# Context copy ahead of the next head's exponential on ScalarE, and output stores issued by SyncE

## The chip, the cores and the metric

The program runs on one core of a Trainium2 chip. The time is device microseconds (us) of one execution. Three timed executions of the kernel before gave 4782.5 us as their median (4778.81 to 4790.28). In the profile the engines are PE (TensorE matmuls), PEld (TensorE weight loads), DVE (VectorE), ACT (ScalarE), POOL (GpSimd) and SP (SyncE, which here only issues DMAs).

## The reference, cut to what matters

The program computes one layer: projections, two kinds of attention (a sliding-window one, "window", and one over at most 256 selected keys, "latent"), a gated mix, and a SwiGLU block. The change lies in the attention. Cut down, the latent branch is:

```python
rel   = relu(einsum('bqhd,bsd->bqhs', q_idx, k_idx))       # index scores, 8 heads
score = einsum('bqh,bqhs->bqs', w_idx, rel)                # masked by chunk, then top_k(score, 256)
q_lat = einsum('bqhd,hrd->bqhr', q, w_uk)                  # "absorbed" query
logits = einsum('bqhr,bqkr->bhqk', q_lat, c_sel) * scale - slope * dist
p   = softmax(logits)                                      # over the selected keys
ctx = einsum('bhqk,bqkr->bqhr', p, c_sel)                  # "context"
o   = einsum('bqhr,hrd->bqhd', ctx, w_uv)
```

The window branch computes a softmax over 16 + 128 keys with a sink, and its product with V. Both outputs go to a DRAM tensor, `attn`, which the last stage reads.

## The kernel before

Four stages follow each other, with a barrier between them: projection, key preparation, `attention` (busy from about 1138 to 2755 us of the profiled execution) and `mix_and_ffn`. Only `attention` is changed.

`attention` works through 16 tiles of 128 queries, and in each tile through 8 heads: 128 steps, n = 8 t + h. A tile t has 16 + 128 (t+1) visible keys, so the steps grow. There is no scheduler: each engine has its own program, written by hand as one loop over n, and the engines meet through semaphores. An engine executes its instructions in order, so whatever waits holds up everything behind it on that engine.

In step n the engines do this:

- **PE**: transposes the first two items of step n (an item is a window piece, in heads 3 to 6, or a group of four key blocks of the latent probabilities), with up to two buffers `turn` in PSUM; then index scores for 32 steps ahead (`index`, tiles up to 11 only); then the first block of logits for step n+2 (`logits`, matmuls at L94 to L96); then `weigh` of item 0, which multiplies the copied transposes with the values (L926 for a window item, L931 for a latent one). It goes on with the transpose of item 2, `weigh` of item 1, the further blocks of logits, and the remaining items. The first latent `weigh` of a step waits for `ctx_free` (the context of step n-1 has been copied out of its only PSUM buffer) and every `weigh` waits for `turn_free` (ACT has copied this item's transposes into `p_t`). In head 0 the step ends with the transpose of the finished window output (L942) and `expand` (L949: context times w_uv for the previous tile); in head 2 with the transpose of the latent output.
- **ACT**: `latent_exp(n+1)` (L1049, waits for DVE's `u_ready`; PE needs it only for the transposes of step n+1); in head 1 `evacuate_product(1, t-1)` (L1079, waits for `expand`); `evacuate_context(n-1)` (L1075, waits until the last `weigh` of step n-1 has ended); in heads 2 to 5 `window_exp` (L1055, L1057); then the first count of the search for the k-th score (`tally`, L1043, which waits for POOL); then `evacuate` of items 0 and 1 (L1069, copies transposes to `p_t`), `rectify` (L1021), the second count, the other items, and the third count. At the end of heads 0 and 2 it runs `store`: a copy of the transposed output into `o_t` (L1088), a drain, and the DMA to `attn` (L1090), issued by ACT itself.
- **DVE** adds distances to logits (L1268), sums index scores, and counts for the search in the even tile of a pair. **POOL** judges each count (L777) and gives the next candidate. The counts run in even tiles (2, 4, ..., heads 1 to 7) and in the first three heads of odd ones, and in tile 0, but not in tiles 14 and 15.
- **SP** loads each tile's inputs: `load_qb`, `load_qi`, `load_window` and `load_values`.

Of the kernel before, what the change touches and what calls it, by code (L numbers as in the profile page):

```python
# [25 lines left out]
P = 128  # L26
# [18 lines left out]
START = 1  # L45
# [11 lines left out]
TILES = SEQ // P  # L57
# [440 lines left out]
def attention(nc, proj, v_nat, w_uk, w_uv, sinks, attn, keys):  # L498
# [4 lines left out]
    with Scope(nc, "at") as s:  # L503
# [59 lines left out]
        sink_used = s.sem("sink_used")  # L563
        stats_a, exp_a, raw_ready, o_ready, attn_stored = s.sem("stats_a"), s.sem("exp_a"), s.sem("raw_ready"), s.sem("o_ready"), s.sem("attn_stored")
        count_ready, sign_ready, cand_ready, kth_ready = s.sems("count_ready"), s.sems("sign_ready"), s.sems("cand_ready"), s.sems("kth_ready")
# [70 lines left out]
        with nc.Block() as block:  # L636
            @block.sync
            def _(sp):
# [31 lines left out]
                def load_values(t):  # L670
# [4 lines left out]
                    sp.dma_start(v_win[:, 1, :], v_nat[w0 + WH - META:w0 + WH - META + WH, :]).then_inc(v_loaded, 16)  # L675

                load_qi(0)
                load_qb(0)
# [4 lines left out]
                for t in range(TILES - 1):  # L683
                    load_qb(t + 1)
                    if t + 5 < TILES:
                        load_qi(t + 5)
                    load_window(t + 1)
                    load_values(t + 1)

            @block.gpsimd  # L690
# [308 lines left out]
            def _(act):  # L999
# [84 lines left out]
                def store(branch, t):  # L1084
                    u, k = turn_at["out", t, branch]
                    act.wait_ge(turn_ready[u], k + 1 + START)
                    act.wait_ge(attn_stored, 32 * t + START)
                    act.activation(o_t[branch][:, :, :], turn[u][:, :].rearrange("p (j q) -> p j q", j=4), ACT.Copy).then_inc(turn_free[u], 1)  # L1088
                    act.drain()
                    act.dma_start(attn[branch * 512:branch * 512 + 512, t * P:t * P + P].rearrange("(j p) c -> p j c", p=P),  # L1090
                                  o_t[branch][:, :, :]).then_inc(attn_stored, 16)

# [7 lines left out]
                for n in range(STEPS):  # L1100
# [5 lines left out]
                    if searches(n, 0):  # L1106
                        orient(q)
                    if n + 1 < STEPS:
                        latent_exp(n + 1)
                    if h == 1 and t:  # L1110
                        evacuate_product(1, t - 1)
                    if n:
                        evacuate_context(n - 1)
                    if searches(n, 0):
                        flip(q)
# [31 lines left out]
                store(1, TILES - 1)  # L1147
                act.wait_ge(attn_stored, 32 * TILES + START)

# [641 lines left out]
```

## Time and profile before

| | |
|---|---|
| Median of three timed executions | 4782.5 us |
| The profiled execution's own time | 4787.24 us |
| Its span in the profile | 4785.4 us |
| PE busy | 3987.3 us (83%) |
| PEld busy | 3309.6 us (69%) |
| ACT busy | 1707.0 us (36%) |
| DVE busy | 1524.6 us (32%) |
| POOL busy | 1534.7 us (32%) |
| Mean granted clock of TensorE | 0.893 of full speed |

An engine's busy time is the union of its instructions' times. In a row of the timeline the first number is the start, the second the duration, both in microseconds; brackets give the engine's idle time just before and what released it. A row with x8 merges eight instructions. Two neighbouring instructions of ACT overlap by about 0.1 us in these rows, so what one occupies of the engine is the distance from its start to the start of the next.

### The profile page before, as it was taken

The page shows a single profiled execution, that of the slowest core. Times are in us where ns is not written, and L with a number is a line of the kernel's source. Part 1 is how long each engine was busy: PE and PEld are TensorE (multiplying, and loading weights), DVE is VectorE, ACT ScalarE, POOL GpSimd, SP SyncE. Part 2 cuts the span into 40 slices and gives each one's busy share as a digit, 9 for nine tenths or more (in the row PEclk, how much of TensorE's full clock was granted, in tenths as well). Part 3 has the DMA queues.
Part 4 walks back from the last instruction along what each step waited for, and adds up shares of the span by engine and source line. Part 5 has one row for each costly group of instructions (what it writes and reads, how often), then busy time and mean ns, then how long its engine had stood idle before and what let it go on. Part 6 is the DMA issues. An engine that isn't in the chain of part 4 may idle for free. (4 is left out here: it accounts for less than half of the span.)

```text
span 4785.4 us, 56614 instructions
## 1 busy us (share of the span) xinstructions
PE 3987.3 (83%) x19153; PEld 3309.6 (69%) x19153; DVE 1524.6 (32%) x2432; ACT 1707.0 (36%) x2775; POOL 1534.7 (32%) x1991
## 2 busy tenths in 40 slices
PE   2999999935677777777778868998899889988998
PEld 2888888714565666666667756886688768876886
DVE  7000000034455666666664213103210331023111
ACT  1000121114556666666664423422242224322221
POOL 2101011023444342323230033444444434453443
PEclk9999999955667888888889988999899989998999
DMA  4111212121100000000000042334233423333332
GB/s 159 53 57 62 66 53 66 57 53 24 31 18 24 25 16 17 17 16 12 12 12 13 7 160 75 96 114 150 70 96 114 132 92 96 115 107 117 96 94 87
DMA packets 368443, 321.21 MB, mean 67 GB/s; under 512 B 18120, under 2 KB 327528, under 8 KB 364168
## 3 DMA queue, kind: packets, MB, share of 16 engines
q1 hardware_dynamic: 344400, 292.72, 20.3%
q10 hardware_dynamic: 23872, 26.29, 1.6%
q8 instruction: 97, 1.59, 0.1%
q14 instruction: 74, 0.61, 0.0%
HBM read 258.79 MB, written 60.17 MB: 67 GB/s over the span
## 5 line engine op out<-in xcount | busy, mean ns | idle before, releaser
L1468 POOL TENSOR_TENSOR ff_w_lo<-ff_raw,ff_w_hi 128x1024 fp32r<-128x1024 f32 x328 | 794.8, 2424 | 1015.3 <-ACT ff_w_hi L1515 1015.3
L94 PE MATMUL ff_bank<-ff_h_hi,ff_w_lo 128*128 128x512 f32 x1664 | 660.4, 397 | 97.1 <-POOL ff_w_lo L1468 81.4
L95 PE MATMUL ff_bank<-ff_h_hi,ff_w_hi 128*128 128x512 f32 x1664 | 656.6, 395 | 0.0
L96 PE MATMUL ff_bank<-ff_h_lo,ff_w_hi 128*128 128x512 f32 x1664 | 655.6, 394 | 0.0
L1515 ACT ACTIVATE ff_w_hi<-ff_raw 128x1024 fp32r<-128x1024 f32 x328 | 345.9, 1055 | 762.2 <-PE ff_bank L96 750.5
L931 PE MATMUL at_ctx<-at_p_t,keys_c_nat 128*128 128x128 f32 (+1 forms) x2432 | 418.7, 321 | 153.2 <-ACT at_p_t L1069 152.2
L931 PEld LDWEIGHTS at_ctx<-at_p_t,keys_c_nat 128*128 128x128 f32 (+1 forms) x2432 | 368.8, 225 | 191.7 <-issue 159.4
L94 PEld LDWEIGHTS ff_bank<-ff_h_hi,ff_w_lo 128*128 128x128 f32 x1664 | 318.1, 191 | 174.7 <-issue 108.4
L94 PE MATMUL in_acc<-pj_h_hi,in_w_lo 128*128 128x512 f32 x1024 | 418.5, 409 | 11.9 <-POOL in_w_lo L300 11.9
L96 PE MATMUL in_acc<-pj_h_lo,in_w_hi 128*128 128x512 f32 x1024 | 416.8, 407 | 0.0
L95 PE MATMUL in_acc<-pj_h_hi,in_w_hi 128*128 128x512 f32 x1024 | 416.5, 407 | 0.0
L94 PE MATMUL ff_bank<-ff_w_hi,ff_f_lo 128*128 128x512 f32 x960 | 374.5, 390 | 7.7 <-POOL ff_w_lo L1468 4.1
L96 PE MATMUL ff_bank<-ff_w_lo,ff_f_hi 128*128 128x512 f32 x960 | 373.6, 389 | 0.0
L95 PE MATMUL ff_bank<-ff_w_hi,ff_f_hi 128*128 128x512 f32 x960 | 373.5, 389 | 0.0
L1043 ACT ACTIVATE at_equal<-at_score,at_cand 128x528 bf16<-128x528 f32 (+6 forms) x217 | 297.9, 1373 | 209.9 <-POOL at_cand L780 152.2
L96 PEld LDWEIGHTS ff_bank<-ff_h_lo,ff_w_hi 128*128 128x128 f32 x1664 | 317.9, 191 | 67.7
L95 PEld LDWEIGHTS ff_bank<-ff_h_hi,ff_w_hi 128*128 128x128 f32 x1664 | 318.2, 191 | 65.5
L1200 DVE TENSOR_SCALAR_CACHE_REDUCE at_greater<-at_score,at_cand 128x400 bf16<-128x400 f32 (+6 forms) x217 | 309.9, 1428 | 111.0 <-POOL at_cand L780 71.2
L300 POOL TENSOR_TENSOR in_w_lo<-in_raw,in_w_hi 128x1024 fp32r<-128x1024 f32 x32 | 76.7, 2399 | 729.6 <-ACT in_w_hi L307 729.6
L1069 ACT ACTIVATE at_p_t<-at_turn 128x512 f32<-128x512 f32 (+4 forms) x416 | 212.6, 539 | 198.1 <-PE at_turn L909 179.8
L858 PE MATMUL at_big_i<-keys_ki_hi,at_qi 128*128 128x512 f32 (+4 forms) x352 | 173.6, 493 | 90.4 <-POOL at_qi L716 73.6
L94 PEld LDWEIGHTS in_acc<-pj_h_hi,in_w_lo 128*128 128x128 f32 x1024 | 200.1, 195 | 59.5 <-issue 12.3
(233 smaller groups left out, 6217.0 us busy)
## 6 DMA issues: line engine op xcount, KB each, us to landing
ff_raw<-in_w_ff_gate SPq DMA_DIRECT2D x88, 512.0 KB, 3.8
ff_raw<-in_w_ff_up SPq DMA_DIRECT2D x88, 512.0 KB, 3.8
ff_raw<-in_w_ff_down SPq DMA_DIRECT2D x88, 512.0 KB, 3.6
proj<-in_row SPq DMA_DIRECT2D x32, 1032.0 KB, 4.7
in_raw<-in_w_in SPq DMA_DIRECT2D x32, 512.0 KB, 5.8
ff_gates<-proj SPq DMA_DIRECT2D x64, 256.0 KB, 2.8
ff_raw<-in_w_out SPq DMA_DIRECT2D x32, 512.0 KB, 3.7
ln_x<-in_x SPq DMA_DIRECT2D x16, 512.0 KB, 3.2
```

The source lines that it names most:

```text
L94: pe.matmul(out, lhs_lo, rhs_hi, start=start, stop=False)
L95: pe.matmul(out, lhs_hi, rhs_hi, start=False, stop=False)
L96: return pe.matmul(out, lhs_hi, rhs_lo, start=False, stop=stop)
L300: pool.tensor_tensor(w_lo[u][:, :, :], raw[u][:, :, :], f32(w_hi[u][:, :, :]), ALU.subtract).then_inc(lo_ready[u], 1)
L858: pe.matmul(big_i[:, a:a + n], qi_2[:, h, :], ki_hi[:, cols], start=True, stop=False)
L931: last = pe.matmul(ctx[:, 0, :], c_nat[0:rows, a:a + P], p_t[v][0:rows, m, :], start=(a == 0), stop=(a + rows == w))
L1043: act.activation(equal[:, 0:width(t)], score_of(t), ACT.Sign, bias=one(cand, 1), accum_out=one(count, 1)).then_inc(count_ready[1], 1)
L1069: act.activation(p_t[v][0:rows, 0:many, :], turn[u][0:rows, 0:many * P].rearrange("p (m q) -> p m q", m=many), ACT.Copy).then_inc(turn_fre ...
L1200: dve.tensor_scalar(greater[:, 0:width(t)], score_of(t), one(cand, 0), None, ALU.is_ge, ALU.add, accum_out=one(count, 0)).then_inc(count_r ...
L1468: pool.tensor_tensor(w_lo[u][:, :], raw[u][:, :], f32(w_hi[u][:, :]), ALU.subtract).then_inc(lo_ready[u], 1)
L1515: act.activation(w_hi[u][:, :], raw[u][:, :], ACT.Copy).then_inc(hi_ready[u], 1)
```

## The change

On ACT, `latent_exp(n + 1)` moves behind `evacuate_product(1, t - 1)` and `evacuate_context(n - 1)`. And the DMA of `store` moves to SP: ACT only counts up a new semaphore `out_ready` after the drain, and SP waits for it. SP's stores of tile t-1 stand between `load_window(t + 1)` and `load_values(t + 1)`, those of the last two tiles at the end, and so does the wait for their landing, which ACT had before.

```diff
+                def store(branch, t):
+                    sp.wait_ge(out_ready, 2 * t + branch + 1 + START)
+                    sp.dma_start(attn[branch * 512:branch * 512 + 512, t * P:t * P + P].rearrange("(j p) c -> p j c", p=P),
+                                 o_t[branch][:, :, :]).then_inc(attn_stored, 16)
...
                     load_window(t + 1)
+                    if t:
+                        store(0, t - 1)
+                        store(1, t - 1)
                     load_values(t + 1)
+                for t in (TILES - 2, TILES - 1):
+                    store(0, t)
+                    store(1, t)
+                sp.wait_ge(attn_stored, 32 * TILES + START)
...
                     act.drain()
-                    act.dma_start(attn[branch * 512:branch * 512 + 512, t * P:t * P + P].rearrange("(j p) c -> p j c", p=P),
-                                  o_t[branch][:, :, :]).then_inc(attn_stored, 16)
+                    act.sem_inc(out_ready, 1)
...
-                    if n + 1 < STEPS:
-                        latent_exp(n + 1)
                     if h == 1 and t:
                         evacuate_product(1, t - 1)
                     if n:
                         evacuate_context(n - 1)
+                    if n + 1 < STEPS:
+                        latent_exp(n + 1)
...
-                act.wait_ge(attn_stored, 32 * TILES + START)
```

ACT's instructions at the end of tile 15's head 0 and the start of its head 1, before (`at_o_t` is the output's copy, `at_u_b` the exponential, `at_o_nat` the product's copy, `at_ctx_t` the context's, `at_p_t` the copies that `weigh` reads):

```order
L1069 ACTIVATE at_p_t<-at_turn 16x128
L1088 ACTIVATE at_o_t<-at_turn 128x512
L1090 DMA attn<-at_o_t 128x4x128
L1049 ACTIVATE at_u_b,at_den_b<-at_u_b,at_min_b 128x2064
L1079 ACTIVATE at_o_nat<-at_misc 128x512
L1075 ACTIVATE at_ctx_t<-at_ctx 128x128
L1069 ACTIVATE at_p_t<-at_turn 128x512 x4
```

The same place on ACT in the changed kernel, where the lines have moved by 12:

```order
L1081 ACTIVATE at_p_t<-at_turn 16x128
L1100 ACTIVATE at_o_t<-at_turn 128x512
L1091 ACTIVATE at_o_nat<-at_misc 128x512
L1087 ACTIVATE at_ctx_t<-at_ctx 128x128
L1061 ACTIVATE at_u_b,at_den_b<-at_u_b,at_min_b 128x2064
L1081 ACTIVATE at_p_t<-at_turn 128x512 x4
```

The DMA is gone from ACT, and the exponential, which was first, is now behind the copy that waits for `expand` and the one that waits for the last `weigh`.

ACT at the start of tile 15's head 4, before:

```order
L1069 ACTIVATE at_p_t<-at_turn 16x128
L1049 ACTIVATE at_u_b,at_den_b<-at_u_b,at_min_b 128x2064
L1075 ACTIVATE at_ctx_t<-at_ctx 128x128
L1057 ACTIVATE at_u_a,at_den_a<-at_u_a,at_bias_a 128x208 x2
L1069 ACTIVATE at_p_t<-at_turn 104x512
```

And in the changed kernel:

```order
L1081 ACTIVATE at_p_t<-at_turn 16x128
L1087 ACTIVATE at_ctx_t<-at_ctx 128x128
L1061 ACTIVATE at_u_b,at_den_b<-at_u_b,at_min_b 128x2064
L1069 ACTIVATE at_u_a,at_den_a<-at_u_a,at_bias_a 128x208 x2
L1081 ACTIVATE at_p_t<-at_turn 104x512
```

The two have changed places; the first copy that `weigh` reads (104x512) stays behind both.

## Rows read from the trace of the kernel before

**Rows 1.** Three stretches: length, then busy time of each engine, PEclk, DMA share, GB/s.

```profile
1138.00:2300.00 1162.00, 846.69 (x4589) 720.95 (x4590) 718.98 (x1121) 710.56 (x1388) 433.56 (x1226) 0.79 0.07 19
2300.00:2549.00 249.00, 187.31 (x1141) 166.65 (x1140) 161.81 (x187) 153.53 (x239) 65.03 (x203) 0.85 0.05 13
2549.00:2765.00 216.00, 174.55 (x1249) 153.48 (x1247) 52.16 (x96) 93.59 (x182) 16.41 (x17) 0.96 0.06 21
```

**Rows 2.** Waits from 1138 to 2765 us: total us, times, longest.

```profile
POOL at_step L777 <- DVE at_greater L1200: 253.2, 98, 8.5
...
PE at_ctx L931 <- ACT at_p_t L1069: 152.2, 48, 9.3
```

**Rows 3.** Context copy: durations (ns); ACT's idle before it; who waited (us, times).

```profile
L1075 ACT ACTIVATE at_ctx_t<-at_ctx x128: 250/256/279, 1148.5 to 2746.4; 128x128 f32<-128x128 f32 x128
...
  PE at_ctx L931: 6.2, 7
...
  PEld at_ctx L931: 127.3, 27
```

**Rows 4.** Timeline of PE and ACT, tile 8, head 4 to 5: start, duration.

```profile
1900.09 1.74 PE L931 MATMUL at_ctx<-at_p_t,keys_c_nat 128*128 128x128 f32 x12
...
1903.82 1.26 ACT L1049 ACTIVATE at_u_b<-at_u_b,at_min_b 128x1168 f32<-128x1168 f32 x1
```

**Rows 5.** Timeline of PE and ACT, tile 15, head 3 to 4.

```profile
2704.85 1.47 PE L931 MATMUL at_ctx<-at_p_t,keys_c_nat 128*128 128x128 f32 x10
...
2705.22 2.00 ACT L1049 ACTIVATE at_u_b<-at_u_b,at_min_b 128x2064 f32<-128x2064 f32 x1
...
2707.22 0.25 ACT L1075 ACTIVATE at_ctx_t<-at_ctx 128x128 f32<-128x128 f32 x1
...
2708.28 1.05 ACT L1069 ACTIVATE at_p_t<-at_turn 104x512 f32<-104x512 f32 x2
...
2708.91 1.10 PE L926 MATMUL at_misc<-at_v_win,at_p_t 104*128 104x64 f32 x8 [0.18 <-ACT at_p_t L1069]
```

**Rows 6.** The same in tile 14, head 3 to 4.

```profile
2602.37 2.20 PE L931 MATMUL at_ctx<-at_p_t,keys_c_nat 128*128 128x128 f32 x16
...
2603.07 1.90 ACT L1049 ACTIVATE at_u_b<-at_u_b,at_min_b 128x1936 f32<-128x1936 f32 x1
...
2606.02 1.07 ACT L1069 ACTIVATE at_p_t<-at_turn 104x512 f32<-104x512 f32 x2
...
2606.82 1.00 PE L926 MATMUL at_misc<-at_v_win,at_p_t 104*128 104x64 f32 x8
```

**Rows 7.** Timeline of PE and ACT, tile 15, end of head 0 and head 1.

```profile
2665.98 1.90 PE L949 MATMUL at_misc<-at_wuv,at_ctx_t 128*128 128x64 f32 x16
...
2666.84 0.38 ACTq L1090 DMA_DIRECT2D attn<-at_o_t  x1
2667.27 2.02 ACT L1049 ACTIVATE at_u_b<-at_u_b,at_min_b 128x2064 f32<-128x2064 f32 x1 [0.49 <-issue]
...
2669.29 0.58 ACT L1079 ACTIVATE at_o_nat<-at_misc 128x512 f32<-128x512 f32 x1
...
2670.05 0.28 ACT L1075 ACTIVATE at_ctx_t<-at_ctx 128x128 f32<-128x128 f32 x1 [0.18 <-issue]
2670.22 1.08 ACT L1069 ACTIVATE at_p_t<-at_turn 128x512 f32<-128x512 f32 x2
...
2670.95 1.13 PE L931 MATMUL at_ctx<-at_p_t,keys_c_nat 128*128 128x128 f32 x8 [0.80 <-ACT at_p_t L1069]
```

**Rows 8.** Timeline of PE and ACT, tile 15, end of head 2 and head 3.

```profile
2692.64 2.02 ACT L1049 ACTIVATE at_u_b<-at_u_b,at_min_b 128x2064 f32<-128x2064 f32 x1 [0.50 <-issue]
...
2696.44 0.74 PE L926 MATMUL at_misc<-at_v_win,at_p_t 104*128 104x64 f32 x5 [2.13 <-ACT at_p_t L1069]
```

**Rows 9.** Timeline of PE and ACT, tile 9, head 7.

```profile
2048.90 1.49 ACT L1049 ACTIVATE at_u_b<-at_u_b,at_min_b 128x1424 f32<-128x1424 f32 x1 [2.89 <-DVEq L1271]
...
2051.28 0.91 PE L931 MATMUL at_ctx<-at_p_t,keys_c_nat 128*128 128x128 f32 x6 [0.51 <-ACT at_p_t L1069]
```

More of the change, by code:

```diff
@@ L563, in attention @@
         sink_used = s.sem("sink_used")
-        stats_a, exp_a, raw_ready, o_ready, attn_stored = s.sem("stats_a"), s.sem("exp_a"), s.sem("raw_ready"), s.sem("o_ready"), s.sem("attn_stored")
+        stats_a, exp_a, raw_ready, o_ready, out_ready, attn_stored = s.sem("stats_a"), s.sem("exp_a"), s.sem("raw_ready"), s.sem("o_ready"), s.sem("out_ready"), s.sem("attn_stored")
         count_ready, sign_ready, cand_ready, kth_ready = s.sems("count_ready"), s.sems("sign_ready"), s.sems("cand_ready"), s.sems("kth_ready")
```

## The prediction

> **What bounds the kernel now.** I read the busy time by stretch first, then the waits of the attention stage, then the timeline of ACT and PE side by side. The first view shows that in the attention no engine is full: from 1138 to 2300 us PE is busy 846.7 of 1162 us, and DVE and ACT about 710 each [rows 1]. So the time is a chain that goes from engine to engine. From 2549 us (tiles 14 and 15) PE is busy 174.6 of 216 us and ACT 93.6. The waits say where the chain changes engine: PE stood 152.2 us in 48 places before a latent `weigh` until ACT had made `p_t`, and POOL 253.2 us in 98 places for DVE's count [rows 2]. PE waits for `p_t`; what ACT does ahead of the first `p_t` copy of a step is therefore on the path, unless PE still has logits to do.
>
> **What the exchange does in one step.** Both copies and the exponential stand ahead of the first `p_t` copy in both orders, so no work leaves that piece; only where ACT waits can change. The exponential waits for DVE's `u_ready`, the context copy for PE's last `weigh` of the step before, and the head-1 product copy for `expand`. Three cases follow.
>
> (1) Both inputs are long there when ACT arrives. Tile 8's head 4 is typical: the last `weigh` ended at 1900.09 + 1.74 = 1901.83, the exponential began at 1903.82 [rows 4]. The exchange costs nothing. I compared the 128 steps one by one; in some 80, nearly all steps with a search, it is so.
>
> (2) ACT arrives before PE has finished. Before, the exponential covered that wait: ACT idled only 6.2 us in 7 of 128 steps ahead of the context copy [rows 3]. Now ACT waits first and then does the exponential. Tile 15, head 4: the exponential began at 2705.22, while the last `weigh` ended at 2704.85 + 1.47 = 2706.32. The new exponential begins at 2706.32 + 0.03 (semaphore) + 0.16 (what the copy occupies), and the copy's 0.16 behind it is saved, so everything behind both is late by 2706.35 - 2705.22 = 1.13 us. PE's L926 already waited (0.18) for the `p_t` copy [rows 5], so PE loses the whole 1.13. In tile 14 the same reckoning gives 2602.37 + 2.20 + 0.03 - 2603.07 = 1.53; PE had 2606.82 - 2606.55 - 0.1 = 0.17 us of cover there (first copy's end 2606.55 from two copies in 1.07 us at 2606.02, 0.1 the usual hop), which leaves 1.36 [rows 6].
>
> The steps where PE is then late, each reckoned like this: tile 15, heads 2, 4, 5, 6: 4 x 1.13 = 4.5. Tile 14, heads 4 and 5: 2 x 1.37; head 2: 0.7; heads 6 and 7, where PE's logits cover about 1.0 of 1.53: 2 x 0.55; 4.5 together. Tile 13, heads 2, 5, 6: 0.3 + 1.3 + 0.45 = 2.1. Five small ones in tiles 1, 5, 6 and 10: 1.0. In tiles 3, 5, 11 and the rest of 1, ACT is late by 0.2 to 0.7 too, but PE's index scores and logits cover it (0.5 to 4 us), so nothing. Sum: +12.1 us.
>
> Head 1 is its own place. The product copy now comes before the exponential and needs `expand`, which in tile 15 ends at 2665.98 + 1.90 = 2667.88. Then 0.03 + 0.76 (product copy with its drain, 2670.05 - 2669.29) + 0.17 (context, 2670.22 - 2670.05) + 2.02 (exponential with its read, 2669.29 - 2667.27) give 2670.86 for the first `p_t` copy, against 2670.22 before: +0.64, and PE waited 0.80 for it [rows 7]. Tiles 4 to 12 (even), 14 and 15 read alike at 0.62 to 0.69, tile 2 with 0.3 left after its cover: 7 x 0.65 + 0.3 = +4.9 us. In odd tiles to 13 `expand` ends 2 to 5 us before ACT gets there: nothing.
>
> (3) DVE is late: ACT waits for `u_ready` and the context is ready. Then the context copy slips into the wait and its 0.16 goes off the path. Tile 9's head 7 is such a step: 2.89 us of wait for DVE, and PE waited 0.51 for `p_t` [rows 9]. There are nine with PE waiting (tiles 7, 9, 11, 13): 9 x -0.16 = -1.4 us.
>
> **The stores.** ACT's gap between the output copy and the next instruction is 0.49 to 0.50 us, of which the DMA issue takes 0.38 [rows 7, 8]. With drain and semaphores alone the gap is 0.18 (behind the product copy, the row of L1075 in rows 7). So 0.32 us can go per store. It does go where nothing else is late: after head 2 in tiles 3 to 15, 13 times; in head 3 of tile 15 PE waited 2.13 us for ACT [rows 8]. After head 0 it goes nowhere: in even tiles and 15 the product copy now waits for `expand`, in odd ones the count waited 0.8 to 4 us for POOL anyway. The last two stores change only who issues. 13 x -0.32 = -4.2 us; the bounds are 0 and 32 x -0.38 = -12.2. On SP the stores hold up `load_values(t+1)`, which waits for head 6 anyway, later than the store's head 2, and the next tile's loads stand behind that: no cost. The transfers are the same, so no bandwidth changes (the DMA share is 0.05 to 0.07 [rows 1]). [...]
>
> **Sum.** 12.1 + 4.9 - 1.4 - 4.2 = +11.4 us. The profiled execution took 4787.24 and would become 4798.6; it lay 4.7 above the median of the three timed ones, so I put the change on the median: 4782.5 + 11.4 = 4794.
>
> **The rivals.**
> - *Absorbed.* The delays of ACT are real, but the chain through DVE and POOL gives most of them back: in the search steps POOL waits for DVE's count (253.2 us [rows 2]), not for ACT's. Against it: tiles 14 and 15 have no search, and there PE waits for ACT directly [rows 5]. If a third of the 17.0 us comes through: 5.7 - 1.4 - 4.2 = about 0: 4783. At zero it is 4777.
> - *Context gate, the faster side.* PEld waited 127.3 us in 27 places for the context copy [rows 3]. If that single PSUM buffer is what holds PE, the copy comes earlier by one exponential, 1.26 to 2.0 us [rows 4, 5], say 1.3 x 27 = 35 us, and with the stores the time is 4782.5 - 35 - 4.2 = 4743. It decides only if the context copy is the last thing PE needs. Against it: it is only the weight load that waits there; the matmul needs `p_t`, which ACT makes after the context copy in both orders, and all rows of PE's matmuls name `p_t` as the releaser [rows 5, 7, 9].
> - *The clock falls.* [...] If the new waits bring the last stretch to 0.85, its 174.6 us of PE become 174.6 x 0.96/0.85 = 197, +22 if all of it is on the path, about half of that by the share of steps bound by ACT: 11.4 + 12 = 4806. Against it: PE's 2.13 us wait in tile 15 [rows 8] is longer than the new ones of about 1.3. [...]
>
> That SP does not issue the stores in time is no case of its own: a tile passes before `o_t` is reused.
>
> **Chances.** Forecast 0.53 (own range 4788 to 4800), absorbed 0.27, clock 0.14, context gate 0.06. The range 4779 to 4808 takes in the forecast, nearly all of absorbed and the clock's middle. A measurement of this kernel tells from no change what is over about 0.2%, 9.6 us; the forecast's 11.4 is just beyond it, and two thirds of its cases are. Slower: 0.53 x 0.63 + 0.14 = 0.48 with rounding. Same: 0.53 x 0.37 + 0.27 less a little = 0.45. Faster: 0.07.
>
> **What would show it.** In the changed profile ACT's idle before the context copy should grow from 6.2 us in 7 steps to some 40 to 60 us in about 40, most in tiles 13 to 15; the idle of PE before L926 and L931 in tile 15's heads 4 and 5 from 0.2 to about 1.3, and each of those steps 1.1 us longer; the gap behind the output copy from 0.49 to about 0.18. The step in head 1 of the even tiles should be 0.6 longer. If tiles 14 and 15 together are not 9 to 11 us longer, the reckoning of case (2) is wrong; if tiles 2 to 12 move by more than some 5 us either way, it is the clock or the search chain, which I did not resolve; if the context copies come earlier and PE's matmuls with them, the gate was real.

## The result and the profile after

| | Kernel before | Changed kernel |
|---|---|---|
| Median | 4784.66 us (8 runs, 4778.81 to 4790.28) | 4805.4 us (8 runs, 4795.36 to 4808.05) |
| Span of the profiled execution | 4785.4 us | 4803.6 us |
| Mean granted clock of TensorE | 0.893 | 0.892 |
| ACT busy | 1707.0 us | 1707.9 us |

The changed kernel takes 1.0040 times as long (95% interval 1.0029 to 1.0051): +20.7 us. It was timed again in a later series and gave 4803.65 against 4787.69, 1.0031 (1.0019 to 1.0043): +16.0 us. The forecast was +11.4. No engine has more work (PE x19153, DVE x2432, ACT x2775 and POOL x1991 instructions in both traces; PE busy 3987.3 us before and 3991.2 us after), so nearly all of the time is in waits. Differences in us are those of the medians. The ratio and its interval are estimated from all the runs, so the two can lie some us apart.

Busy time by stretch, changed kernel, columns as in [rows 1]. The third stretch ends later, since the attention does:

```profile
1138.00:2300.00 1162.00, 845.02 (x4546) 719.03 (x4545) 715.67 (x1116) 705.68 (x1381) 429.82 (x1226) 0.78 0.07 18
2300.00:2549.00 249.00, 185.29 (x1165) 164.42 (x1165) 163.29 (x190) 157.08 (x245) 63.75 (x203) 0.88 0.05 13
2549.00:2784.00 235.00, 181.09 (x1268) 158.03 (x1267) 53.23 (x98) 95.37 (x183) 16.40 (x17) 0.94 0.08 25
```

The waits between 1138 and 2784 us, changed kernel (who waited, for whom: us in total, times, longest):

```profile
POOL at_step L789 <- DVE at_greater L1210: 252.9, 98, 7.0
PE at_ctx L943 <- ACT at_p_t L1081: 157.9, 50, 9.3
PE at_misc L938 <- ACT at_p_t L1081: 103.7, 48, 5.4
ACT at_ctx_t L1087 <- PE at_ctx L943: 55.2, 43, 4.3
ACT at_u_b L1061 <- DVEq L1281: 33.9, 10, 8.9
```

The fourth row is the new one. ACT's wait ahead of the context copy was 6.2 us in 7 steps [rows 3] and is 55.2 us in 43. PE's wait before a latent `weigh` rose from 152.2 to 157.9 us, and before a window `weigh` (third row) from 100.9 to 103.7, while POOL's wait for DVE's count stayed (253.2 before [rows 2]). So most of the new 49 us is no new idle time on the path: ACT used to arrive later at the same wait, having done the exponential in it. The last row was 59.8 us in 24 places before: a part of ACT's waiting for DVE is now spent, or covered, ahead of it. Of the 55.2 us, 27.0 are in tiles 13 to 15, so about half, where the prediction said most.

The context copy by its source line, changed kernel:

```profile
L1087 ACT ACTIVATE at_ctx_t<-at_ctx x128: 254/267/279, 1148.7 to 2761.8; 128x128 f32<-128x128 f32 x128
...
  PE at_ctx L943: 55.2, 43
...
  PEld at_ctx L943: 108.6, 18
```

The last row is the weight loads that waited for this copy: 127.3 us in 27 places before [rows 3], 108.6 in 18 now. They wait less, and the kernel is slower all the same.

Tile 15, end of head 3 and start of head 4, timeline of the changed kernel (start, duration, engine; idle before in brackets), the place of [rows 5]:

```profile
2715.18 1.47 PE L943 MATMUL at_ctx<-at_p_t,keys_c_nat 128*128 128x128 f32 x10
...
2716.69 0.28 ACT L1087 ACTIVATE at_ctx_t<-at_ctx 128x128 f32<-128x128 f32 x1 [1.04 <-PE at_ctx L943]
2716.87 2.01 ACT L1061 ACTIVATE at_u_b<-at_u_b,at_min_b 128x2064 f32<-128x2064 f32 x1
...
2719.77 1.06 ACT L1081 ACTIVATE at_p_t<-at_turn 104x512 f32<-104x512 f32 x2
...
2720.40 0.77 PE L938 MATMUL at_misc<-at_v_win,at_p_t 104*128 104x64 f32 x5 [1.33 <-ACT at_p_t L1081]
```

ACT stands 1.04 us until the last `weigh` (2715.18 + 1.47 = 2716.65) is over, copies, and only then starts the exponential. PE's idle before its first `weigh` went from 0.18 [rows 5] to 1.33, and the step is 1.17 us longer; 1.13 was reckoned. Tile 14's head 4 is the same picture, with the place of [rows 6]:

```profile
2604.11 2.20 PE L943 MATMUL at_ctx<-at_p_t,keys_c_nat 128*128 128x128 f32 x16
...
2606.35 0.28 ACT L1087 ACTIVATE at_ctx_t<-at_ctx 128x128 f32<-128x128 f32 x1 [1.44 <-PE at_ctx L943]
...
2609.95 1.10 PE L938 MATMUL at_misc<-at_v_win,at_p_t 104*128 104x64 f32 x8 [1.23 <-ACT at_p_t L1081]
```

Tile 15, head 1 (the place of the first of [rows 7]), and then the end of head 2, behind which the latent output is stored [rows 8]; both changed kernel:

```profile
2673.31 1.90 PE L961 MATMUL at_misc<-at_wuv,at_ctx_t 128*128 128x64 f32 x16
...
2674.17 0.41 SPq L679 DMA_DIRECT2D attn<-at_o_t  x1
...
2675.24 0.60 ACT L1091 ACTIVATE at_o_nat<-at_misc 128x512 f32<-128x512 f32 x1 [1.14 <-PE at_misc L961]
...
2678.93 0.80 PE L943 MATMUL at_ctx<-at_p_t,keys_c_nat 128*128 128x128 f32 x5 [1.45 <-ACT at_p_t L1081]
...
2700.65 0.60 ACT L1100 ACTIVATE at_o_t<-at_turn 128x512 f32<-128x512 f32 x1 [1.63 <-PE at_turn L954]
...
2701.31 0.41 SPq L679 DMA_DIRECT2D attn<-at_o_t  x1
...
2701.37 0.28 ACT L1087 ACTIVATE at_ctx_t<-at_ctx 128x128 f32<-128x128 f32 x1
```

In head 1 PE waits 1.45 us for `p_t`, 0.80 before [rows 7]: the forecast's 0.65. Behind the output copy ACT goes on after 2701.37 - 2701.25 = 0.12 us, where it needed 0.50 [rows 8]. SP issues the store 0.06 us after the copy's end.

For each step I took the end of its last latent `weigh` in both traces, and from two neighbours the step's length. The differences, changed kernel less kernel before:

| Tile, head | Forecast | Measured |
|---|---|---|
| 15, heads 2, 4, 5 | 1.13 each | 1.15, 1.17, 1.15 |
| 15, head 6 | 1.13 | 2.75 |
| 15, heads 0 and 3 | 0 and -0.32 | 1.22 and 1.23 |
| 15 and 14, head 1 | 0.65 each | 0.61, 0.65 |
| 14, heads 2, 4, 5 | 0.7, 1.37, 1.37 | 0.73, 1.52, 1.49 |
| 14, heads 6, 7 | 0.55 each | 0.62, 0.75 |
| 14, heads 3 and 0 | -0.32 and 0 | -0.38 and -1.56 |
| 13, heads 2, 5, 6 | 0.3, 1.3, 0.45 | 0.00, -0.31, 0.51 |
| Tiles 14 and 15 together | 4.5 + 4.5 + 2 x 0.65 - 2 x 0.32 = 9.7 | 13.1 |
| All up to the end of tile 13 | the rest of the 11.4: 1.7 | 2.3 |
| All that follows the attention | 0 | 2.8 |

The last three rows sum to 18.2, which is 4803.6 - 4785.4. The 1.2 to 1.6 us by which tile 15's heads 0, 3 and 6 exceed the forecast come with a lower granted clock: over these three steps it is 0.82, 0.90 and 0.85, where it was 0.90, 1.00 and 1.00 before. In tile 14's head 0, 1.56 us shorter, it is 1.00, where it was 0.88. The other steps of the two tiles have 1.00 in both traces and lie within 0.2 us of the forecast. Such jumps stand in the tiles before too, up or down and at other steps in other traces: tile 4's head 0 is 3.35 us longer here, with the clock at 0.68, and 0.02 shorter in experiment 5's trace of the same kernel, with the clock at 1.00 as before. So the sum up to tile 13 says little. Two windows of tile 15, changed kernel (columns as above), and matmuls of the same shape from each:

```profile
2747.00:2751.00 4.00, 3.90 (x22) 3.76 (x22) 0.00 (x0) 0.82 (x2) 0.00 (x0) 0.62 0.01 4
2751.00:2755.00 4.00, 4.00 (x35) 3.86 (x33) 0.00 (x0) 1.46 (x3) 0.00 (x0) 0.96 0.00 0
```

```profile
2746.79 1.10 PE L938 MATMUL at_misc<-at_v_win,at_p_t 104*128 104x64 f32 x8 [1.84 <-ACT at_p_t L1081]
...
2748.90 1.92 PE L943 MATMUL at_ctx<-at_p_t,keys_c_nat 128*128 128x128 f32 x8
...
2751.41 1.05 PE L943 MATMUL at_ctx<-at_p_t,keys_c_nat 128*128 128x128 f32 x8
```

With the granted clock at 0.62 (0.50 from 2749 to 2750.8 us, within the eight matmuls), eight matmuls took 1.92 us, with it at 0.96 they took 1.05. What went before the fall is PE's idle time of 1.84 us; at the same place of the kernel before it was 0.67 us, the granted clock stayed at 1.00 and the eight matmuls took 1.06. That the longer wait is the cause is not shown: experiment 3 has such a fall without a longer wait. From 2660 to 2765 us the granted clock is 0.94, from 2653 to 2750 in the trace of before it was 0.98.

### The profile page after: what moved, and what is told of

Read it like the earlier page. It is cut to its first block and busy times, and to the rows that moved or that the text cites. A ratio compares the mean times of both kernels' runs of the same rounds, so it can differ in the third digit from the quotient of the medians.

```text
span 4803.6 us, 56615 instructions
## 1 busy us (share of the span) xinstructions
PE 3991.2 (83%) x19153; PEld 3311.4 (69%) x19153; DVE 1525.7 (32%) x2432; ACT 1707.9 (36%) x2775; POOL 1528.8 (32%) x1991
## 5 line engine op out<-in xcount | busy, mean ns | idle before, releaser
L943 PE MATMUL at_ctx<-at_p_t,keys_c_nat 128*128 128x128 f32 (+1 forms) x2432 | 420.0, 322 | 158.8 <-ACT at_p_t L1081 157.9
L94 PEld LDWEIGHTS in_acc<-pj_h_hi,in_w_lo 128*128 128x128 f32 x1024 | 199.9, 195 | 58.9 <-issue 12.1
```

The lines of the kernel that those rows point to most:

```text
L94: pe.matmul(out, lhs_lo, rhs_hi, start=start, stop=False)
L943: last = pe.matmul(ctx[:, 0, :], c_nat[0:rows, a:a + P], p_t[v][0:rows, m, :], start=(a == 0), stop=(a + rows == w))
```

## The experiments

The first four kernels were timed beside 27 runs of the kernel before (4787.56 us), the next four beside 17 (4787.69), the last four beside 20 (4788.83).

**1. The exchange alone.** The order of the changed kernel, but ACT still issues its stores:

```diff
-                    if n + 1 < STEPS:
-                        latent_exp(n + 1)
                     if h == 1 and t:
                         evacuate_product(1, t - 1)
                     if n:
                         evacuate_context(n - 1)
+                    if n + 1 < STEPS:
+                        latent_exp(n + 1)
```

> The order of the changed kernel on ScalarE, but the output stores issued by ScalarE as before. Path theory (ScalarE's waits for PE before the first p_t copy are uncovered, the stores give back 13 x 0.32 us): slower than before by the prediction's 12.1 + 4.9 - 1.4 = 15.6 us at least, and by up to 25 us if the whole measured loss of about 21 us plus the stores' 4.2 belongs to the exchange. Rival (the surplus over the forecast comes from SyncE issuing the stores): about +11 to +16 us, less than the changed kernel. ScalarE's idle before the context copy about 55 us in 43 places, as in the changed kernel.

Measured: 4803.27 us (5 runs), 1.0037 (1.0024 to 1.0051), +15.7. The forecast's terms for the exchange, 12.1 + 4.9 - 1.4, are 15.6. The value lies in the bands of both expectations, so it doesn't decide between them. Nor is the agreement as good as it looks: in the trace, tiles 14 and 15 are 13.7 us longer, where 10.3 were reckoned without the stores, and all up to tile 13 is 0.6 longer, where 5.3 were. Two misses, +3.4 and -4.7, largely cancel.

The trace shows what became of the 2.1 us of tile 13: it is 0.2 us longer. First the kernel before in head 5, then, in the second block, the exchange alone:

```profile
2520.65 1.01 PE L926 MATMUL at_misc<-at_v_win,at_p_t 104*128 104x64 f32 x8
...
2534.26 0.90 PE L909 MATMUL at_turn<-at_ident,at_u_b 128*128 128x128 f32 x3 [7.03 <-DVE at_ql_lo L1278]
```

```profile
2522.13 1.10 PE L926 MATMUL at_misc<-at_v_win,at_p_t 104*128 104x64 f32 x8 [1.12 <-ACT at_p_t L1069]
...
2534.45 0.90 PE L909 MATMUL at_turn<-at_ident,at_u_b 128*128 128x128 f32 x3 [5.65 <-DVE at_ql_lo L1278]
```

The new wait of 1.12 us is there, but PE waits later in the same step for something that ACT's order doesn't move, and that wait is 1.38 us shorter. The step ends 0.07 us later than before, where 1.3 were reckoned.

**2. The stores alone.** The changed kernel with the exponential first again:

```diff
+                    if n + 1 < STEPS:
+                        latent_exp(n + 1)
                     if h == 1 and t:
...
-                    if n + 1 < STEPS:
-                        latent_exp(n + 1)
```

> The order of before on ScalarE, only the output stores issued by SyncE. Path theory: 13 stores give 0.32 us each, -4.2 us (bounds 0 and -12.2); the gap behind the output copy falls from 0.49 to about 0.18. Rival (stores on SyncE cost something, by its queue or by collisions): 0 to +10 us.

Measured: 4783.8 us (11 runs), 0.9994 (0.9985 to 1.0003), -3.8; forecast -4.2. The interval includes no change, so the time alone doesn't show the gain. The trace does. From the end of tile 15's head 2, this kernel:

```profile
2689.41 0.60 ACT L1100 ACTIVATE at_o_t<-at_turn 128x512 f32<-128x512 f32 x1 [1.63 <-PE at_turn L954]
2690.07 0.41 SPq L679 DMA_DIRECT2D attn<-at_o_t  x1
2690.13 2.02 ACT L1061 ACTIVATE at_u_b<-at_u_b,at_min_b 128x2064 f32<-128x2064 f32 x1
...
2693.93 1.08 PE L938 MATMUL at_misc<-at_v_win,at_p_t 104*128 104x64 f32 x8 [1.75 <-ACT at_p_t L1081]
```

PE's wait fell from 2.13 [rows 8] to 1.75 us: the whole issue of 0.38 us. Thirteen such stores would give 4.9. And with the exponential first, the store after head 0 is won as well: head 1 of tiles 4 to 14 (even) and 15 is 0.19 to 0.43 us shorter, 2.4 in sum. The forecast's -4.2 counted none of these, since in the changed kernel the product copy waits there. So for this kernel its own reckoning gives about -7 us, near the end of the interval (-7 to +1), and that -3.8 is near -4.2 is partly chance.

**3. The old order in the last three tiles.** From the changed kernel:

```diff
+                    if t >= 13 and n + 1 < STEPS:
+                        latent_exp(n + 1)
                     if h == 1 and t:
...
-                    if n + 1 < STEPS:
+                    if t < 13 and n + 1 < STEPS:
                         latent_exp(n + 1)
```

> The changed kernel with the old order in tiles 13 to 15 only. Path theory: the loss sits where no search runs. It takes back the 11.1 us of tiles 13 to 15 and 1.3 us of the two head-1 places there, and the two extra drops of the clock in tile 15 (some 3 us): 12 to 16 us below the changed kernel, that is +5 to +9 us against before. Rival (the surplus lies in the search tiles, or the clock there): at most 8 us below the changed kernel, +12 us or more against before.

Measured: 4791.08 us (11 runs), 1.0012 (1.0003 to 1.0021), +3.5, a little less than the +5 to +9 expected. Tiles 14 and 15 together are 0.1 us longer than before instead of 13.1. In these tiles ACT's order and the stores are those of experiment 2, whose trace has them 1.6 us shorter than before; nearly all the rest is a fall of the clock in tile 15's head 3. The same `weigh` in that head, first in this kernel and then, in the second block, in experiment 2's:

```profile
2699.71 1.91 PE L943 MATMUL at_ctx<-at_p_t,keys_c_nat 128*128 128x128 f32 x8
```

```profile
2695.28 1.06 PE L943 MATMUL at_ctx<-at_p_t,keys_c_nat 128*128 128x128 f32 x8
```

PE's wait at the start of that head is 1.75 us in both. The granted clock is 0.50 around the first (2699 to 2702 us) and 1.00 around the second (2695 to 2697).

**4. The old order in head 1 only.** From the changed kernel:

```diff
                     if h == 1 and t:
+                        if n + 1 < STEPS:
+                            latent_exp(n + 1)
                         evacuate_product(1, t - 1)
...
-                    if n + 1 < STEPS:
+                    if n + 1 < STEPS and not (h == 1 and t):
                         latent_exp(n + 1)
```

> The changed kernel, but in head 1 the exponential stays first and the product copy and the context copy follow it, as before. Path theory: head 1 alone is 0.62 to 0.69 us in seven tiles and 0.3 in one, so 4.9 us below the changed kernel, and step by step head 1 of tiles 4 to 14 (even) and 15 is 0.6 shorter. Rival (search steps absorb it): 0 to 2 us below.

Measured: 4794.05 us (11 runs), 1.0017 (1.0008 to 1.0027), +6.5. That is 9.5 us less than the changed kernel's +16.0 in the other series. It is also nearly twice the 4.9 us that were expected, and the traces say why. Head 1 of tiles 14 and 15 goes from +0.65 and +0.61 to -0.40 and -0.41, so about 1.05 for each, and tiles 4 to 12 (even) show 0.8 to 1.0: the 0.65 that was reckoned, and up to 0.38 of the store after head 0, which can only be won where the product copy doesn't wait. Over the seven steps and tile 2 that is about 7 us; the remaining 2 us or so lie within the intervals.

**5. The changed kernel again**, with no edit, to know the size:

> The changed kernel unaltered, beside the kernels of this series. If exchange and stores simply add, it is 15.7 - 3.8 = +12 us against before, by their measured medians, and not the +20.7 of its first series. Path theory with additive parts: +9 to +15. Rival (the two parts meet, the stores' gain in the head-3 steps lost or the clock of tile 15 worse in this combination): +17 to +24.

Measured: 4803.65 us (6 runs), 1.0031 (1.0019 to 1.0043), +16.0. Its trace has tiles 14 and 15 at +3.80 and +9.29 us (the first had +3.82 and +9.28), and the same steps long in tile 15. All up to the end of tile 13 came to +5.5 (+2.3 in the first), the part behind the attention to -0.2 (+2.8). So the surplus in tile 15 came again in this kernel; what lies elsewhere changes from execution to execution. The +16.0 lies between the two bands that were expected.

**6. The context copied twice**, in the kernel before, to price a delay that sits in front of every first `p_t` copy:

```diff
+                    act.activation(spare_t[:, :], ctx[:, 0, :], ACT.Copy)
                     act.activation(ctx_t[:, n % HEADS, :], ctx[:, 0, :], ACT.Copy).then_inc(ctx_free, 1)
```

> The kernel before, with the context copied a second time into a spare buffer just ahead of its copy, in all 128 steps: 0.16 us more on ScalarE ahead of the first p_t copy, wherever it is. Path theory: TensorE waits for p_t in 48 + 44 places, so 92 x 0.16 = +15 us. Absorbed theory (the search chain gives it back): 0 to +5 us, from tiles 14 and 15 alone.

Measured: 4804.59 us (6 runs), 1.0034 (1.0022 to 1.0046), +16.9. A copy that occupies 0.16 us costs 16.9 / 128 = 0.13 us per step on average, and the interval (+11 to +22 us) leaves out the 0 to +5 of the absorbed theory. But the trace doesn't show that every step pays. Of the 128 steps 36 are 0.10 to 0.20 us longer, among them six of tile 15 and, in search tiles, head 1 of tiles 2 to 12 (even); 44 steps move by less than 0.07. The steps that differ by less than 0.45 us sum to +5.2. The rest lies in jumps of one to three us, some of which stand in traces of experiments 2, 9 and 10 at the same steps without any cause in the edit (tile 4's head 0: +2.46 here, +2.47 in experiments 2 and 9, with the granted clock at 0.75 in all three where it was 1.00 before). Where the other 12 us come from is not shown.

**7. Both copies late, the exponential first.** From the changed kernel, with `ctx_t` doubled:

```diff
-                    if h == 1 and t:
-                        evacuate_product(1, t - 1)
-                    if n:
-                        evacuate_context(n - 1)
                     if n + 1 < STEPS:
                         latent_exp(n + 1)
+                    if n and not 3 <= h < 7:
+                        evacuate_context(n - 1)
...
-                    for item in items[:2]:
+                    for i, item in enumerate(items[:2]):
                         evacuate(item)
+                        if 3 <= h < 7 and i == 0:
+                            evacuate_context(n - 1)
+                    if h == 1 and t:
+                        evacuate_product(1, t - 1)
```

> Stores on SyncE, the exponential first as in the kernel before, and the copies that TensorE does not wait for moved behind the p_t copies: in heads 3 to 6 the context copy behind item 0's, and in head 1 the product copy behind those of items 0 and 1 (the buffer of the copied contexts is doubled, so that head 1 can overwrite none that expand still reads). Path theory: 44 waits before L926 x 0.16 = -7, 14 x 0.76 = -10.6 in head 1, stores -3.8: about -21 us against before. Absorbed theory: -4 to -8.

Measured: 4779.09 us (11 runs), 0.9983 (0.9974 to 0.9992), -8.6. Less than half of what was expected. In tile 9 head 1 gained 2.02 us (with the granted clock at 0.89 instead of 0.80) and head 2 gave 1.68 back: PE's wait for `p_t` there rose from 3.72 to 5.21 us. Tile 7 shows -0.61, then +2.55, but 1.57 of that stands in experiment 2's trace as well. So a saving in a search tile can be absorbed. Of the 0.16 us per context copy, tile 15's heads 4 to 6 show the whole and tile 14's nothing (+0.03, 0.00, +0.01). The order with the context copy behind a first latent copy wasn't tried.

**8. The exponential behind the first copies of the step**, all else ahead of it. From the changed kernel, with `ctx_t` doubled:

```diff
-                    if h == 1 and t:
-                        evacuate_product(1, t - 1)
                     if n:
                         evacuate_context(n - 1)
-                    if n + 1 < STEPS:
-                        latent_exp(n + 1)
...
                     for item in items[:2]:
                         evacuate(item)
+                    if h == 1 and t:
+                        evacuate_product(1, t - 1)
                     if nb_i:
                         rectify(m, 0)
+                    if n + 1 < STEPS:
+                        latent_exp(n + 1)
```

> As the one with late copies, but with the context copy first and the exponential of the next head behind the p_t copies of items 0 and 1 and the first rectify, in head 1 behind the product copy too. It takes 1.3 to 2.0 us per step from what stands ahead of p_t. Path theory: TensorE's 253 us of waits for p_t in 92 places shrink by 1.2 to 1.9 each where they are that long: -60 to -120 us against before, less what the uncovered waits for the last weigh (55 us) give back, which in this order TensorE's own next transposes cover. Absorbed theory: the searches bind (253 us of GpSimd's waits for VectorE's count), -20 us or less, only from tiles 13 to 15. A third way: the exponential delays the following p_t copies and the gain is gone, 0 +/- 5.

Measured: 4743.1 us (4 runs), 0.9907 (0.9892 to 0.9922), -44.6. Tile 15, start of head 4, this kernel:

```profile
2674.81 0.28 ACT L1087 ACTIVATE at_ctx_t<-at_ctx 128x128 f32<-128x128 f32 x1 [1.04 <-PE at_ctx L943]
...
2675.89 1.07 ACT L1081 ACTIVATE at_p_t<-at_turn 104x512 f32<-104x512 f32 x2
...
2676.84 2.02 ACT L1061 ACTIVATE at_u_b<-at_u_b,at_min_b 128x2064 f32<-128x2064 f32 x1
...
2677.03 1.00 PE L938 MATMUL at_misc<-at_v_win,at_p_t 104*128 104x64 f32 x8
```

ACT waits the same 1.04 us for PE as in the changed kernel, but now the 2 us exponential no longer follows between that wait and the copies, and PE's `weigh` begins with no idle time. The gain was smaller than the 60 us or more expected. It lies mostly in tiles 10 (-8.3), 12 (-11.3), 14 (-5.7) and 15 (-5.3). It is not the exponential's alone: the stores on SP and the late product copy are in it. Experiment 7, which has both and the exponential first, gave -8.6, so the exponential's new place is worth about 36 us. Tile 14's heads 4 to 7 did not move at all (0.0 against before), so something else sets those steps once ACT is out of the way.

**9. Two buffers for the context**, in the kernel before, the test of the gate:

```diff
-                        pe.wait_ge(ctx_free, n + START)
+                        pe.wait_ge(ctx_free, max(n - 1, 0) + START)
...
-                            last = pe.matmul(ctx[:, 0, :], c_nat[0:rows, a:a + P], p_t[v][0:rows, m, :], start=(a == 0), stop=(a + rows == w))
+                            last = pe.matmul(ctx[:, n % 2, :], c_nat[0:rows, a:a + P], p_t[v][0:rows, m, :], start=(a == 0), stop=(a + rows == w))
...
-                    act.activation(ctx_t[:, n % HEADS, :], ctx[:, 0, :], ACT.Copy).then_inc(ctx_free, 1)
+                    act.activation(ctx_t[:, n % HEADS, :], ctx[:, n % 2, :], ACT.Copy).then_inc(ctx_free, 1)
```

> The kernel before with two context buffers in PSUM used in turn, so that a step's first latent weigh waits for the context copy of the step before last only. ScalarE's order and the stores are those of before. Gate theory (TensorE's 127 us of weight-load waits for the context copy are on the path): 27 places, about -35 us. Path theory (p_t releases TensorE, and it comes later than the context copy in any case): 0, within 3 us; the weight load may start earlier, the matmul not.

Measured: 4793.29 us (11 runs, 4779.42 to 4796.6), 1.0000 (0.9991 to 1.0009). The medians differ by +4.5 us, the interval is -4 to +4, and -35 is far outside. The context copy by its source line, this kernel:

```profile
L1075 ACT ACTIVATE at_ctx_t<-at_ctx x128: 250/258/282, 1149.7 to 2755.5; 128x128 f32<-128x128 f32 x128
...
  PEld at_ctx L931: 125.1, 26
```

`weigh` no longer waits for the copy of the step just before, and yet the view still puts 125.1 us of weight-load waiting down to it (127.3 before [rows 3]). The view names the last event that it saw, not what held PE. The gate is refuted. This trace also warns of what one trace can hide: with ACT's order unchanged it is 9.7 us longer than the kernel before up to the end of tile 13, nearly all in jumps of the kind named above (the steps in which the granted clock was at 0.50 for over 1 us more or less than before sum to +9.2), and within 0.6 us of it in tiles 14 and 15.

**10. The new order in the last three tiles only**, in the kernel before:

```diff
-                    if n + 1 < STEPS:
+                    if t < 13 and n + 1 < STEPS:
                         latent_exp(n + 1)
...
                         evacuate_context(n - 1)
+                    if t >= 13 and n + 1 < STEPS:
+                        latent_exp(n + 1)
```

> The kernel before with the new order in tiles 13 to 15 only, stores issued by ScalarE. Path theory: the same loss there as in the exchange alone, whose tiles 13 to 15 were 0.2 + 7.3 + 6.4 = 13.9 us longer in its trace, all of it: +12 to +16 us. If the loss in these tiles depended on what the exchange does in tiles 0 to 12, it would be under 8.

Measured: 4803.35 us (10 runs), 1.0028 (1.0018 to 1.0037), +14.5, as expected. In its trace ACT's wait for the context is 31.3 us in 22 places, tiles 14 and 15 are 7.4 and 12.6 us longer, and tile 13 is 0.4 shorter. From both sides, then (experiment 3 takes the loss away, this one makes it there alone), nearly all of the loss is in the last three tiles, and by the traces in tiles 14 and 15, which have no search. They lose more than in the changed kernel (19.9 us for 13.1); falls of the clock are part of it, since the granted clock from 2660 to 2690 us is 0.77 there, where it was 0.94 before.

**11. The first count behind the copies as well.** From experiment 8's kernel:

```diff
-                    for r in rounds[:1]:
-                        tally(q, r)
                     for item in items[:2]:
                         evacuate(item)
+                    for r in rounds[:1]:
+                        tally(q, r)
```

> The kernel with the late exponential, and also the first count of each search step behind the p_t copies of items 0 and 1. Path theory (TensorE's waits for p_t set the search tiles too; 143 us of them are left in 45 places before L943): -20 to -50 us against the late exponential alone, all in tiles 0 to 13. Search theory (the rounds between ScalarE, VectorE and GpSimd set those tiles, so that the count must not come later): 0 to +30 us.

Measured: 4726.98 us (4 runs), 0.9869 (0.9854 to 0.9884), -61.8; the fastest kernel here. The waits from 1138 to 2740 us, this kernel:

```profile
POOL at_step L789 <- DVE at_greater L1210: 183.4, 90, 6.9
...
PE at_ctx L943 <- ACT at_p_t L1081: 122.3, 47, 6.1
...
PE at_misc L938 <- ACT at_p_t L1081: 27.6, 15, 6.0
```

PE's wait for latent `p_t` copies fell from 152.2 to 122.3 us, and POOL's for DVE from 253.2 to 183.4 [rows 2]. Tiles 10 to 13 gained 11.8, 6.2, 13.1 and 9.4 us against the kernel before. About 17 us beyond experiment 8 is just short of the band expected.

**12. The exponential further back still**, behind items 2 and 3. From experiment 8's kernel:

```diff
-                    if n + 1 < STEPS:
-                        latent_exp(n + 1)
                     for r in rounds[1:2]:
                         tally(q, r)
                     for item in items[2:4]:
                         evacuate(item)
+                    if n + 1 < STEPS:
+                        latent_exp(n + 1)
```

> The kernel with the late exponential, and the exponential still further back, behind the p_t copies of items 2 and 3, where ScalarE idled 4.1 us in each step of tile 15. Path theory: in tiles 14 and 15 the copies of items 2 and 3 come up to 1 us earlier but TensorE did not wait for them (0.4 us of ScalarE's idle time before them), so little there: -2 to 0 us; in the search tiles the second count and items 2 and 3 come up to 1.5 us earlier: 0 to -25 us. It is worse only if the exponential then ends after TensorE asks for it: +5 to +20.

Measured: 4768.68 us (5 runs), 0.9959 (0.9946 to 0.9973), -20.2, so about 24 us worse than experiment 8: outside what was expected. The waits from 1138 to 2740 us, first this kernel's and then, in the second block, those of experiment 8's:

```profile
PE at_ctx L943 <- ACT at_p_t L1081: 125.6, 38, 8.1
...
PE at_turn L921 <- ACT at_u_b L1061: 30.3, 16, 4.0
```

```profile
PE at_ctx L943 <- ACT at_p_t L1081: 143.2, 45, 7.7
...
PE at_misc L938 <- ACT at_p_t L1081: 70.0, 30, 6.6
```

PE's wait for `p_t` is 17.6 us shorter, but its transposes now wait 30.3 us in 16 places for the exponential itself, a wait that experiment 8's kernel does not have. The exponential has a due time, the next step's transposes. None of the 16 places is in tiles 14 and 15, which gained nearly as much as in experiment 8 (5.6 and 4.8 us); all up to tile 13 gained 9.1 us instead of 33.9. The waits shown make up only a part of the 24 us. POOL's wait for DVE's count also rose, from 233.1 to 256.9 us, so the search chain may have a share, and no run tells the two apart.

## Why the prediction was right, and where its size was off

Direction and range were right: slower, by +16.0 to +20.7 us where 11.4 were forecast, and 4805.4 lies in the range 4779 to 4808, near its upper end, outside the forecast's own range of 4788 to 4800. Of the signs that it named, two came out against it: tiles 14 and 15 are 13.1 us longer and not 9 to 11 (10.2 without the jumps of the clock), and tiles 2 to 12 moved by +4.1 us in one trace and +6.9 in the other, where the limit was 5, by such jumps: the steps in which the granted clock was at 0.50 for over 1 us more or less than before sum to +6.4 and +7.0 us, the others to -2.4 and -0.2.

- **Case (2), ACT waits first, +12.1.** Right in its mechanism where no search runs: 1.15, 1.17 and 1.15 for 1.13 in tile 15, and PE's idle 1.33 as foreseen. Experiments 3 and 10 show that nearly all of the loss is there. Wrong in tile 13: of its 2.1 us only 0.5 came, in head 6. The reckoning looked at PE's wait before the first `weigh` of a step and not at PE's next waits. In head 5 a later wait of 7.03 us for DVE took the delay up (experiment 1), the absorption that the rival spoke of. Tile 14's heads 4 and 5 cost 1.5 instead of 1.37: the 0.17 us of cover taken off was not there, and the whole 1.53 came through.
- **Head 1, +4.9.** Right where no fall of the clock lies beside it: 0.61 to 0.65 in tiles 6, 8, 10, 14 and 15. Tiles 4 and 12 show 3.11 and 2.22 in the first trace, with the granted clock at 0.62 and 0.88, but tile 4 0.63 in experiment 5's and tile 12 0.59 in experiment 1's, with it at 1.00 as before. Its price beside the stores is up to 1.05, as experiment 4 shows, since it also cancels the store's saving. In tiles 8 and 12 head 2 gave back 0.32 and 0.23 (experiment 1).
- **Case (3), -1.4.** It is there: ACT's waits for DVE ahead of the exponential are 33.9 us in 10 places in the changed kernel. Tile 9's head 7 now has the context copy inside such a wait, and PE waits 0.33 where it waited 0.51 [rows 9]. Experiment 1's trace, which has no jumps from tile 8 to tile 13, shows its size: with one in tile 7, seven steps of tiles 7, 9, 11 and 13 are 0.15 to 0.19 us shorter, -1.2 in sum.
- **Stores, -4.2.** About right: 0.38 instead of 0.32 us for one, after head 2, in most of the 13 places (0.33 to 0.38 shorter in tiles 5, 7, 9, 10 and 14, but nothing in tiles 3 and 8). Experiment 2's -3.8 is no measurement of this term, since that kernel wins the stores after head 0 too. What the traces show as won is the 0.38 us of the issue and no more (PE's wait of 2.13 us became 1.75 in experiment 2).
- **Mis-sized: the clock at nothing in the sum.** In the sum every step was reckoned at the clock of before; the clock's fall was a rival with 0.14. It fell in part, though the new waits are not shown to be the cause: experiment 3 has none of them in tile 15 and has a fall in head 3 all the same, and experiment 2, with the same order there and the same wait of 1.75 us, has none. The falls in these two tiles go with 1.2 to 1.6 us of a step each: head 6 of tile 15 was 2.75 instead of 1.15, head 3 was 1.23 instead of -0.38, head 0 was 1.22 instead of 0, and tile 14's head 0 lost the fall that it had before (-1.56). Together +2.9, of the 3.4 us by which tiles 14 and 15 exceed the forecast. The rival's 0.96 and 0.85 are the granted clocks of the last two stretches of [rows 1], and that all of PE's time grows by their ratio was its estimate (eight matmuls took 1.92 us around 0.50 and 1.06 at 1.00). Its level of 0.85 did not come (0.94), nor its 22 us.
- **The parts together.** Taken one at a time, +15.7 and -3.8 give +11.9, but together they measured +16.0 and +20.7. A part of the gap is an interaction that the traces show: head 1 of tile 14 is +0.64 with the exchange alone, -0.38 with the stores alone and +0.65 with both. The store's saving there is lost behind the wait for `expand`, and over tiles 4 to 14 (even) and 15 it is the 2.4 us of experiment 2. The forecast had this in its terms (it counted 13 stores), the sum of the two experiments has not. So that +11.9 is so near +11.4 is chance.
- **Not settled.** The rest of the gap, 1.7 to 6.4 us, lies within the intervals of experiment 1 (+11 to +24 us), experiment 2 (-7 to +1) and experiment 5 (+9 to +21). After the attention, traces of one and the same kernel differ by 3 us, and up to tile 13 traces in which nothing acts there differ by up to 9.7 us (experiment 9). I can't name what decides that.
- **Rivals.** Absorbed: wrong as a whole, since the loss in tiles 14 and 15 comes through and experiment 6's +16.9 is beyond its band, but true in single search steps, for a delay in tile 13's head 5 (experiment 1) and for savings (experiment 7). Context gate: refuted by experiment 9. The two readings of one row, "PEld waits for the context copy" and "the matmul waits for `p_t`", were told apart by the matmul's row, and that was the right one.

## What to carry to other kernels

On an engine that works in order, as ACT does here (in tile 15's head 4 the exponential starts only behind the copy that waits 1.04 us), an instruction whose input comes late belongs behind work that can cover the wait, and work for which nobody waits yet belongs behind what somebody waits for. Here moving a waiting 0.16 us copy ahead of a 2 us exponential cost 0.3 to 0.4%, and moving exponential, count and product copy behind the awaited copies, with the stores on SyncE, gained 1.3%, up to the point where the exponential itself came due (experiment 12). A delay that is read off one wait is lost only if no later wait in the same step takes it up: in tile 13's head 5 the new wait of 1.12 us was followed by one that fell from 7.03 to 5.65 us (experiment 1). Before a buffer is doubled, look at whether the matmul or only the weight load waits for it: here it was the weight load, 127.3 us, and the second buffer gave a ratio of 1.0000 (experiment 9).

## What the runs showed of the hardware that was not expected

- In tile 15 short falls of the granted clock come at the same steps in two traces of the changed kernel (+9.28 and +9.29 us), at 1.2 to 1.6 us each, and at others in other kernels. The one in head 6 has 0.50 from 2748.0 to 2751.3 us. From about head 0 of tile 15 on the granted clock is 0.98 before (2653 to 2750 us) and 0.94 after (2660 to 2765 us). But of the four steps with the new idle time only one had a fall (head 6 with 0.85; heads 2, 4 and 5 have 1.00), and one came without it: in head 3, behind the same wait of 1.75 us, experiment 3 had a fall (0.50) and experiment 2 had none (1.00).
- A copy that the profile shows with 0.26 us, and with 0.16 us to the next instruction's start, cost 0.13 us per step of the program's time on average (experiment 6), and its trace accounts for less than half of that.
- A wait of the weight load that the profile puts down to a copy (125.1 us) was worth nothing that could be measured when what it named was taken away (experiment 9: 1.0000, 0.9991 to 1.0009).
